# Twelve of 48 modulation units leave the layers of a two-block transformer and are multiplied later

## The reference, cut to what matters

```python
for layer in range(DEPTH):                                    # DEPTH = 2, N_MOD = 6, D_MODEL = 1024
    mod   = (silu(c)     @ ada_w[layer] + ada_b[layer])[:, None, :]   # ada_w[layer]: 1024 x 6144, float32
    mod_c =  silu(c_ctx) @ ada_w[layer] + ada_b[layer]
    sh1, sc1, g1, sh2, sc2, g2 = split(mod, 6)                # the same six for mod_c
    h = rms_norm(x, norm1_g[layer]) * (1 + sc1) + sh1
    ...                                                       # mixer or attention gives y
    x = x + g1 * y
    x = x + g2 * conv_ffn(rms_norm(x, norm2_g[layer]) * (1 + sc2) + sh2, ...)
```

## Time and profile before

| what | value |
|---|---|
| time, median of 3 runs | 1655.83 us (1655.11 to 1657.88) |
| span of the profiled execution | 1639.1 us |
| that median less the span | 16.7 us |
| PE busy | 1588.8 us, 97% |
| PEld busy | 1499.5 us, 91% |
| DVE busy | 962.9 us, 59% |
| ACT busy | 759.7 us, 46% |
| POOL busy | 133.8 us, 8% |
| 48 modulation loads | 1 MB each, median 7.5 us to landing |

### The profile page before, as it was taken

One profiled execution on the slowest core, in us unless ns is written; L12 is line 12 of the kernel. 1 busy time (PEld: TensorE's weight loads), 2 busy tenths in 40 slices (PEclk: granted clock), 3 DMA queues, 4 the chain that ended last, 5 costly groups with the idle time before them and its releaser, 6 DMA issues.

```text
span 1639.1 us, 32148 instructions
## 1 busy us (share of the span) xinstructions
PE 1588.8 (97%) x13979; PEld 1499.5 (91%) x13979; DVE 962.9 (59%) x1200; ACT 759.7 (46%) x1146; POOL 133.8 (8%) x101
## 2 busy tenths in 40 slices
PE   7999999999999999999999999999999999989998
PEld 6998998999989998889899999999998896889998
DVE  6888566477886666555247443344445347767674
ACT  5554554445455544454246332233235336665453
POOL 0330000002220000100010000000010102100000
PEclk9999999999999999999999999999999999989999
DMA  7776656676775666823113323422325334255753
GB/s 265 232 237 217 213 185 219 229 252 210 248 227 189 208 213 201 287 94 104 52 48 108 104 80 89 129 86 87 89 92 170 94 104 91 66 152 152 223 176 121
DMA packets 330077, 259.91 MB, mean 159 GB/s; under 512 B 24017, under 2 KB 322513, under 8 KB 329938
## 3 DMA queue, kind: packets, MB, share of 16 engines
q1 hardware_dynamic: 312002, 252.47, 48.5%
q10 hardware_dynamic: 17936, 5.40, 1.5%
HBM read 256.80 MB, written 1.05 MB: 157 GB/s over the span
## 4 chain that ended last, share of the span: by engine, by line
PE 67%; DVE 15%; issue 9%; ACT 7%; DMA 1%; POOL 1%; ACTq 0%; DVEq 0%; SPq 0%; POOLq 0%
PE banks_g L1277 29%; PE banks_g L878 18%; PE banks_g L1048 4%; PE banks_g L868 4%; DVE w_lo L2321 3%; DVE w_lo L2045 2%; ACT w_hi L1659 2%; PE banks_g L901 2%; PE banks_g L1157 2%; ACT w_hi L1463 1%; PE bank_s L996 1%; PE bank_t L1009 1%; ACT probs L1623 1%; PE bank_t L1324 1%; DVE conv L2446 1%
## 5 line engine op out<-in xcount | busy, mean ns | idle before, releaser
L1277 PE MATMUL banks_g<-h_hi,w_lo 128*128 128x256 f32 x1296 | 360.8, 278 | 2.1 <-DVE h_lo L2512 1.3
L1277 PE MATMUL banks_g<-h_hi,w_hi 128*128 128x256 f32 x1296 | 359.1, 277 | 0.0
L1277 PE MATMUL banks_g<-h_lo,w_hi 128*128 128x256 f32 x1296 | 359.1, 277 | 0.0
L2321 DVE TENSOR_TENSOR w_lo<-raw,w_hi 128x2048 fp32r<-128x2048 f32 (+1 forms) x100 | 208.1, 2081 | 113.9 <-ACT w_hi L1659 113.7
L2045 DVE TENSOR_TENSOR w_lo<-raw,w_hi 128x2048 fp32r<-128x2048 f32 x92 | 211.8, 2302 | 92.2 <-ACT w_hi L1463 92.1
L1277 PEld LDWEIGHTS banks_g<-h_hi,w_lo 128*128 128x128 f32 x1296 | 244.3, 188 | 5.1 <-DVE h_lo L2512 2.1
L1277 PEld LDWEIGHTS banks_g<-h_lo,w_hi 128*128 128x128 f32 x1296 | 244.1, 188 | 0.1
L1277 PEld LDWEIGHTS banks_g<-h_hi,w_hi 128*128 128x128 f32 x1296 | 244.1, 188 | 0.0
L878 PE MATMUL banks_g<-h_hi,w_lo 128*128 128x256 f32 x800 | 227.6, 284 | 0.0
L878 PE MATMUL banks_g<-h_lo,w_hi 128*128 128x256 f32 x800 | 223.1, 279 | 0.0
L878 PE MATMUL banks_g<-h_hi,w_hi 128*128 128x256 f32 x800 | 223.0, 279 | 0.0
(11 more groups left out here) (381 smaller groups left out, 3251.0 us busy)
## 6 DMA issues: line engine op xcount, KB each, us to landing
raw<-w_in SPq DMA_DIRECT2D x76, 1024.0 KB, 5.1
ada_raw<-ada_w SPq DMA_DIRECT2D x48, 1024.0 KB, 7.5
raw<-w_up SPq DMA_DIRECT2D x88, 512.0 KB, 4.5
raw<-w_down SPq DMA_DIRECT2D x32, 704.0 KB, 4.4
raw<-w_branch SPq DMA_DIRECT2D x12, 1024.0 KB, 5.0
raw<-qkv SPq DMA_DIRECT2D x12, 1024.0 KB, 4.9
raw<-w_out SPq DMA_DIRECT2D x8, 1024.0 KB, 5.0
raw<-even_in SPq DMA_DIRECT2D x6, 1024.0 KB, 4.9
```

The source lines that it names most:

```text
L1277: last = nc.tensor.matmul(to, w[:, c, m0:m0 + P], a[:, c, s_ * SEQ:s_ * SEQ + SEQ], start=c == 0 and n == 0, stop=c == kcs - 1 and n == 2)
L2321: nc.vector.tensor_tensor(w_lo[:, u % SLOTS, 0:n], raw[:, u % SLOTS, 0:n], w_hi[:, u % SLOTS, 0:n].bitcast(F32), ALU.subtract).then_inc(dv ...
```

## The change

The layers keep 18 modulation units each (`LAYER_ADA`), counted through both layers' weights, in the places of the first 18 before; the turns take nine units and come after weight units 17 and 37. The last twelve units (the second layer's `sh2`, `sc2`, `g2`) form four groups of 3, 3, 2 and 4. Their products accumulate in one PSUM bank per group, so that ScalarE copies once per group and GpSimd adds nothing. Three turns add the groups' rows. `mod_now` and `ada_bias` go away; the bias is added straight into `mod`. Three further buffers take loads (`late_raw1` and `late_raw2` over `conv` and `hidden` and what is behind them, `late_raw3` in `f_lo`), with a semaphore each.

```diff
-ADA_UNITS = 24
-PACK = 12
-S_AT = 2 * (PACK - 1)
+LAYER_ADA = 18
+PACK = 9
+LATE_ADA = 12
+S_AT = 2 * (LATE_ADA - 1)
...
-        if n % 2 == 0:
+        if n % 2 == 0 and ada[0] < LAYER_ADA:
             ada_unit()
-        if n == 2 * PACK - 1:
-            order.append(("ada turn", 0))
+        if n in (2 * PACK - 1, 4 * PACK + 1):
+            order.append(("ada turn", int(n > 2 * PACK)))
...
-    order = [("ctx turn", b) for b in range(4)] + [("final sums",)]
-    order += [("ctx h", 0), ("ctx h", 1), ("ctx split", 0), ("ctx h", 2), ("final root",), ("ctx h", 3), ("ctx split", 1),
+    order = [("ctx turn", b) for b in range(4)] + [("late ada", 0, 0), ("final sums",)]
+    order += [("late ada", 0, 1), ("late ada", 0, 2), ("ctx h", 0), ("ctx h", 1), ("ctx split", 0), ("ctx h", 2), ("final root",), ("ctx h", 3), ("ctx split", 1),
...
+                if (layer, grp, j) == (1, 0, 1):
+                    order.append(("late turn", 2))
...
     ffn(0)
+    order += [("late ada", 1, 0), ("late ada", 1, 1), ("late ada", 1, 2)]
     order.append(("unit", "nq", 0))
...
-    between = {"nk0": [("qk sum", "q", 0), ("qk sum", "q", 1)],
-               "nk1": [("qk spread", "q", 0), ("qk squares", "k", 0)],
+    between = {"nk0": [("late turn", 0), ("late ada", 2, 0), ("late ada", 2, 1), ("qk sum", "q", 0), ("qk sum", "q", 1)],
+               "nk1": [("late turn", 1), ("qk spread", "q", 0), ("qk squares", "k", 0)],
...
-    norm("11", 0)
+    order += [("late ada", 3, 0), ("late ada", 3, 1), ("norm sum", "11", 0), ("late ada", 3, 2),
+              ("norm spread", "11", 0), ("late ada", 3, 3)]
+    chunks("11", 0, 0, KC)
...
+        LATE_COUNT = (3, 3, 2, 4)
+        LATE_FIRST = (0, 3, 6, 8)
...
+            return (bank_m[:, 0:256], bank_m[:, 0:256], bank_o[:, 0:256], bank_s[:, 0, :])[grp]
...
+                    if u == 44 and layer == DEPTH - 1:
+
+                        sp.wait_ge(pe_steps, pe_.at(f"ada{LAYER_ADA - 1}"))
+                        late_load(0, 0)
+
+                        sp.wait_ge(dve_steps, dve_.at("o lo15"))
+                        late_load(0, 1)
+                        late_load(0, 2)
...
+                if (kind, i) == ("nq", 0):
+
+                    sp.wait_ge(pe_steps, pe_.at("late ada0"))
+                    late_load(1, 0)
+                    sp.wait_ge(dve_steps, dve_.at(f"f lo0 {FC - 1}"))
+                    late_load(1, 1)
+                    late_load(1, 2)
+                if (kind, i) == ("nk", 0):
+
+                    sp.wait_ge(pe_steps, pe_.at("late ada1"))
+                    late_load(2, 0)
+                    late_load(2, 1)
+                if (kind, i) == ("wo", 3):
+
+                    sp.wait_ge(pe_steps, pe_.at("late ada2"))
+                    late_load(3, 0)
+                    sp.wait_ge(pe_steps, pe_.at("sumsqk1"))
+                    late_load(3, 3)
+                if (kind, i) == ("up1", 0):
+
+                    sp.wait_ge(pe_steps, pe_.at("near values15"))
+                    late_load(3, 1)
+                    late_load(3, 2)
                 slot = raw[:, u % SLOTS, :]
...
+                elif what == "late ada":
+
+                    grp, i = arg
...
+                    where = late_of[grp, i]
+                    pe.wait_ge(late_loaded[where], late_value(grp, i))
...
+                    for c in range(KC):
+                        r = slice(32 * (c % 4), 32 * (c % 4) + 32)
+                        last = nc.tensor.matmul(to[r, :], s_cols[:, c, s0:s0 + 32], aw[:, c, :],
+                                                start=i == 0 and c < 4, stop=i == LATE_COUNT[grp] - 1 and c >= 4)
...
+                elif what == "late ada" and arg[1] == LATE_COUNT[arg[0]] - 1:
+
+                    grp = arg[0]
...
+                    act.wait_ge(pe_steps, pe_.at(f"late ada{grp}"))
+                    nc.scalar.activation(late_to[grp][:, :], late_bank(grp), ACT.Copy
+                                         ).then_inc(act_steps, act_.step(f"late row{grp}"))
```

More of the change, by code:

```diff
@@ L88, in constants @@
     t["pick"] = pick
-    parts = np.zeros((P, 2 * PACK), np.float32)
+    parts = np.zeros((P, 2 * LATE_ADA), np.float32)
     for grp in range(4):
-        for r in range(2 * PACK):
+        for r in range(2 * LATE_ADA):
             parts[32 * grp + r, r] = 1.0
@@ L257, in layer_order @@
             order.append(("ctx prep", n - 43))
-        if n == 47:
-            order.append(("ada turn", 1))
-    assert ada[0] == ADA_UNITS
+    assert ada[0] == LAYER_ADA
     return order
@@ L693, in program, with late_bank, late_value, late_turned @@
         CONSTS = 6
+        def late_bank(grp):
+            return (bank_m[:, 0:256], bank_m[:, 0:256], bank_o[:, 0:256], bank_s[:, 0, :])[grp]
+        def late_value(grp, n):
+            where = late_of[grp, n]
+            so_far = [key for key in late_of if late_of[key] == where and key <= (grp, n)]
+            return 16 * len(so_far) + (16 * DEPTH * LAYER_ADA if where == 0 else 0)
+        def late_turned(n):
+            c0, m = ((0, 6), (6, 2), (8, 4))[n]
+            return c0, m, (bank_s[:, 0, 0:4 * m], bank_o[:, 256:256 + 4 * m], bank_o[:, 0:4 * m])[n]
         @block.sync
@@ L1199, in _ @@
                     pe.wait_ge(dve_steps, dve_.at("r12"))
-                    pe.wait_ge(dve_steps, dve_.at("mod now", before=True))
+                    pe.wait_ge(act_steps, act_.at("late row0"))
                     for n in range(2):
@@ L1570, in _ @@
                         act.wait_ge(pe_steps, pe_.at("small", before=True))
-                        act.wait_ge(pool_steps, pool_.at("ada sum23", before=True))
+                        act.wait_ge(pool_steps, pool_.at(f"ada sum{LAYER_ADA - 1}", before=True))
                         nc.scalar.activation(w_small_hi[:, :, :], w_small[:, :, :], ACT.Copy
@@ L2311, in _ @@
                             dve_steps, dve_.step(f"merged lo{q}"))
-                own()
-                nc.vector.tensor_copy(mod[:, layer:layer + 1, :, :], mod_now[:, :, :]
-                                      ).then_inc(dve_steps, dve_.step("mod"))
             enter("end")
@@ L2366, in _ @@
                     low(END_U[tuple(arg)])
+                elif what == "late turn":
+                    n, = arg
+                    c0, units, src = late_turned(n)
+                    dve.wait_ge(pe_steps, pe_.at(f"late turn{n}"))
+                    add_bias(2 * (DEPTH * LAYER_ADA + c0), units, src).then_inc(dve_steps, dve_.step(f"late mod{n}"))
                 elif what == "part" and arg[0] != "vs":
```

102 lines of the change are left out of this document (80 added, 22 removed).

## The result

The changed kernel takes 1676.36 us (median of 4 runs, 1668.91 to 1683.03), the kernel before 1655.47 us beside it (4 runs, 1642.35 to 1657.88): ratio 1.0143, 95% interval 1.0097 to 1.0189. The prediction was 1667.3 us in 1656 to 1675: slower, as forecast, by 20.9 us instead of 11.5.

The account below looks back on a forecast made before the run. TensorE, busy 97% of 1639.1 us, was taken as the bound where it sets the pace. Savings of 8.0 us and costs summed to +11.5, a span of 1650.6; plus 16.7 to the runs' median, 1667.3 us, range 1656 to 1675.

Parts of the forecast that it names:

- 2.7n us later: Weight loads in SP's list: a unit with n late 1 MB loads ahead lands 2.7n us later, at 386 GB/s.
- 1.8 per MB: Attention rounds 4 and 5: tables land after a median 7.7 us beside one 1 MB load, 5.9 without.
- five terms: Late loads' costs at unit 45, `nq0`, `nk0`, the attention tables and `up1 0`: 1.7, 4.8, 2.0, 2.0 and 3.3 us.
- the tables' term: Attention: two late loads ahead of `wo3` delay the tables of rounds 4 and 5; +2.0 us, ends 0 and 5.
- Layers, -8.0: Both layers: six modulation units fewer at each end, less the turns' cost; 8.0 us saved, ends 6.0 and 12.
- Unit 45, +1.7: Layer's end: three late loads ahead of unit 45's make its weights 1.5 to 2 us late; +1.7, ends 0 and 4.
- First group, +0.2 and +2.7: Around the final sums: one unit overfills a hole, +0.2; two units and the copy delay `ctx h`, +2.7.
- Second group, +4.8: At `nq0`: three late loads ahead of its load delay norm and `w_lo`, +4.8 us; the products fill the hole free.
- Third group, +2.6: At `nk0`: two late loads ahead, +2.0 us; products and turn fill the 2.3 us hole, +0.2; second turn +0.4.
- rival 3: Clock: filled holes keep it up, 1663 us, chance 0.07; or new holes lower it, 3 to 7 more, 1672, 0.10.
- Fourth group, +5.5: At `up1 0` and norm `11`: two late loads +3.3 us, third unit and copy +1.8, third turn +0.4.
- rival 4: Dearer: loads a quarter slower (3.4 us per MB) and the fourth group's upper ends; 1674 to 1678 us, chance 0.07.

Follow-up runs that it names:

- the version with the constants later: Kernel with loads spread, copy later and x first in SP's list, its transform matrices and `w_s` loaded behind the second half's first units: 1652.30 us, ratio 0.9970 to before.
- the cut one: The kernel before, with two needless 128-column products ahead of every fourth unit of the first up projection: 1653.57 us, ratio 1.0009.

## Why the prediction was right and wrong

The direction was right, and in every place that it named the mechanism too; the size was not, by more than the result shows. Its own frame was off first: "the profiled span stands 16.7 us under the median of the runs" added a span of the lower group to a median of the upper. Like for like the sum of +11.5 stands against +24 to +28; that the medians differ by only 20.9 us is the luck of how the first four runs of each split over the groups.

The step that failed is the price of a late load in front of a load that someone waits for, "2.7n us later" and "1.8 per MB" beside the tables. Its five terms sum to 13.8 us, and without the loads the kernel is 21 to 26 us faster. The worst of them is the tables' term, +2.0 with ends 0 and 5, where the experiment shows 5.9. Terms put at nothing come on top: the late start, +3.3 to +3.5, and the clock.

Step by step, by the table of stretches:
- Layers, -8.0. Right for TensorE's own share (second layer -3.8 and -3.7 for -3.5). The first layer gave 1.5 us less: the unit behind 42 was rightly worth nothing, but I did not ask what the wider hole does. It brought the clock to 0.50 behind it in this trace and in the second; where the clock stayed up, in the trace of the version with the constants later, the layer gave the 4.5 forecast. The next layer was reached 3.0 us sooner, counted from the later start, not 5.
- Unit 45, +1.7: measured +3.1 and +3.2. The sum of 15.7 us from unit 44's issue to unit 45's landing was 16.9: the first landing came after 5.6 us instead of 4.9, the next four 2.6 to 3.0 apart instead of 2.7; and ScalarE wanted the unit after 13.9 us, not 14.2. SP took 2.1 and 2.6 us to issue the second and third late load, and 2.6 for unit 45's, instead of 0.4; whether that delayed a landing is not shown.
- First group, +0.2 and +2.7: measured +5.0 and +3.8. The copy was nearly right (3.0). The products were priced at the full clock; the first took 1.80 us, the pair 3.21. I had written that the clock drops there and priced the fourth group by it, this one not.
- Second group, +4.8, ends 4.2 and 7: 6.5 by the experiment. 2.7 us per MB is the best rate of the trace, and a load behind three others came 14.8 us after the first issue, not 13.0.
- Third group, +2.6: +2.5 and +0.8. Filling the hole at the query sums was worth more than priced: in the three versions whose loads are spread or left out and that were timed first, this stretch gives 1.3 to 1.4 us, where the forecast had products and turns cost 0.6, and the clock stays up there. So the late load itself costs some 2 to 4 us here, against +2.0. (The page's clock line, on which rival 3 leans, has one digit under 9, at norm `11`; the fall at the query sums shows only in a narrower stretch.)
- Tables, +2.0, ends 0 and 5: 5.9 by the experiment, +4.6 and +5.9 in the two traces of the changed kernel. I took 1.8 us per MB from the difference of two medians; the two halves of round 4's table landed 9.6 and 13.2 us after their issue instead of 6.9 and 8.5, and round 5's 11.5 and 12.6 instead of 6.0 and 7.2. The Trainium skill, page "DMA: Bandwidth & Descriptors", section on queues, rings and completion order, has each DMA engine go round between the queues packet by packet. By an estimate from that rule, half a table, 256 KB in packets of 256 bytes, waits for at most as many packets of 1 KB from SP's queue, 1 MB; it landed 2.7 us later, which is what 1 MB takes, so the trace agrees with the rule. The cap is too high to help.
- Fourth group, +5.5: +7.0 and +6.3. `up1 0` landed 12.6 us after the first late issue, where 10.7 were forecast.
- The start, not in the sum: +3.3 to +3.5. The end, not in the sum either: +0.8 to +1.3, by the slower pitch in the last up projection.

Rival 3's upper half (the new holes bring the clock down more often, 3 to 7 us more) came true in the traces, and with it rival 4 (loads a quarter slower, 3.4 us per MB) in part: 3.2 us per MB at `nq0`, 3.6 at `up1 0`, 2.8 at unit 45. I had kept them apart, as 0.10 and 0.07, and so cut the range at 1675. The Trainium skill, page "TensorE: Matmul & The Clock Gate", section "HAM oscillation", says that waits between bursts bring the clock down; the trace agrees, 47.8 us at the lower level against 20.5. By that rule the holes should have been priced, and I "left the clock as it was". What 27 us more at half the clock cost by themselves was not measured apart from the holes; the layer's end above shows 1.5 us for one such stretch.

Left open: why TensorE takes the one pitch or the other, what exactly SP waits for at the start, and what the late loads of unit 45, `nk0` and `up1 0` cost one by one, which were never put back alone.

## What to carry to other kernels

A prefetch belongs behind the next load that someone waits for, in a stretch with slack, not in front of it where it is first needed: the same twelve megabytes cost over 20 us in front and 0.6 to 3.3 us behind. Work put in a hole is free only if neither its operands' load nor the copy of its result stands ahead of what ends the hole. Before adding a difference of spans to a median, look at whether the runs form groups.

## What the runs showed of the hardware that was not expected

- TensorE follows one 128x256 product with the next at 113.3 or 117.8 ns while the granted clock reads 1.00. In all thirteen uncut traces the pitch holds through the unbroken 330 us of the first up and down projections, where the two values are 13 us apart; in the cut one it changed at each of five cuts by two small products. At many places it is the same in every trace, so it is not all chance: the last up projection has 117.8 ns in eleven traces and 113.3 in the three without the late units ahead of it.
- SP issues nothing for 6.7 to 11.0 us early in all fourteen profiles, from x's issue or one load later until 1.0 to 3.6 us behind x's landing, 1.9 us in nine of them. Whether one load got out ahead of the stall changed between versions that begin SP's list alike, and TensorE's first unit with it by 3 to 5 us. It is not shown that SP waits for its own instructions: no packet of kind "instruction" is listed between 0 and 28 us of any of these traces.
- A load issued behind several others still on their way took SP 2.0 to 4.1 us to issue instead of 0.4 in the worst cases (unit 45, `nq0` and the three loads behind it, `up1 0`).
- Behind a TensorE hole of 2.8 us at the end of the first layer the granted clock fell to 0.50 in 8 of 11 traces, behind one of 1.4 us at the same place in none of three.
